# The fullest expert's overflow tokens in four 32-column tiles of plain fp32

## The reference

```python
def swiglu(x, w1, w3, w2):
    return (jax.nn.silu(x @ w1) * (x @ w3)) @ w2

def moe_ffn(x, router_w, w1, w3, w2):
    logits = (xt @ router_w).astype(F32)
    top_v, top_i = lax.top_k(logits, TOP_K)          # 2 of 8
    top_w = jax.nn.softmax(top_v, axis=-1)
    gates = jnp.sum(jax.nn.one_hot(top_i, N_EXPERTS) * top_w[..., None], axis=1)
    for e in range(N_EXPERTS):
        y = y + gates[:, e:e + 1] * swiglu(xt, w1[e], w3[e], w2[e])
```

## Time and profile before

| | |
|---|---|
| median of three timed runs | 2315.66 us (2313.2 to 2319.87) |
| the profiled execution | 2320.57 us, span 2318.8 us |
| TensorE busy | 98% of the span, 11067 matmul records |
| VectorE, ScalarE busy | 79%, 60% |
| granted TensorE clock, mean | 0.994 |
| DMA | 584.16 MB, mean 252 GB/s |

### The profile page before, as it was taken

How to read it: one execution, slowest core, us unless ns; L and a number is a source line. 1 busy time by engine, 2 the same in 40 slices (tenths; PEclk the granted TensorE clock), 3 DMA queues, 4 the chain that set the end, 5 groups by cost and what they waited for, 6 DMA issues and landing times.

```text
span 2318.8 us, 29142 instructions
## 1 busy us (share of the span) xinstructions
PE 2275.0 (98%) x11067; PEld 1881.2 (81%) x11067; DVE 1824.6 (79%) x2368; ACT 1381.1 (60%) x1580; POOL 31.7 (1%) x44
## 2 busy tenths in 40 slices
PE   8999999999999999999999998999999999999998
PEld 7788887788888788787888876888888888888887
DVE  4965467899867788999899988899765579987655
ACT  4444443578856677788878884565544536644543
POOL 0000000000000000000000000000000000000000
PEclk9999998999999999999999999999999999999999
DMA  8366553699977799999999995644566565355663
GB/s 277 118 209 189 184 167 124 259 348 401 388 245 259 273 341 346 338 409 413 408 373 408 413 413 209 193 128 153 177 195 190 181 202 167 116 184 174 194 187 122
DMA packets 198506, 584.16 MB, mean 252 GB/s; under 512 B 17260, under 2 KB 26616, under 8 KB 183641
## 3 DMA queue, kind: packets, MB, share of 16 engines
q1 hardware_dynamic: 196060, 573.97, 70.4%
q0 software_dynamic: 1872, 6.82, 0.8%
q10 hardware_dynamic: 428, 1.45, 0.2%
HBM read 580.07 MB, written 2.12 MB: 251 GB/s over the span
## 4 chain that ended last, share of the span: by engine, by line
PE 85%; DVE 9%; ACT 2%; issue 2%; DMA 1%; SPq 0%; POOL 0%; DVEq 0%; POOLq 0%; ACTq 0%
PE tile L1051 19%; PE tile L1053 19%; PE tile L1052 19%; PE tile L1572 5%; PE tile L1573 4%; PE aux L1174 3%; DVE units_parts L2578 3%; PE aux L1051 2%; PE aux L1053 2%; PE aux L1052 2%; PE aux L1573 1%; PE aux L1572 1%; PE aux L1543 1%; PE aux L1471 1%; PE aux L1852 1%
## 5 line engine op out<-in xcount | busy, mean ns | idle before, releaser
L2578 DVE TENSOR_TENSOR units_parts<-units,high 128x1024 fp32r<-128x1024 f32 (+3 forms) x339 | 482.5, 1441 | 88.8 <-ACT high L1980 85.9
L1052 PE MATMUL tile<-units_parts,acts 128*128 128x512 f32 (+2 forms) x1344 | 514.9, 383 | 0.0
L1980 ACT ACTIVATE high<-units 128x1024 fp32r<-128x1024 f32 (+3 forms) x339 | 412.4, 1236 | 150.8 <-DMA units<-in_w_ff 42.0
L1051 PE MATMUL tile<-high,acts 128*128 128x512 f32 (+2 forms) x1012 | 402.4, 398 | 5.8 <-DVE units_parts L2578 3.4
L1053 PE MATMUL tile<-high,acts 128*128 128x512 f32 (+2 forms) x1012 | 389.7, 385 | 0.0
L1052 PEld LDWEIGHTS tile<-units_parts,acts 128*128 128x128 f32 x1344 | 254.1, 189 | 47.1 <-issue 2.2
L1051 PEld LDWEIGHTS tile<-high,acts 128*128 128x128 f32 x1012 | 191.4, 189 | 44.1 <-issue 5.5
L1053 PEld LDWEIGHTS tile<-high,acts 128*128 128x128 f32 x1012 | 191.0, 189 | 38.6
L1052 PE MATMUL tile<-units_parts,zbuf_parts 128*128 128x512 f32 x328 | 127.6, 389 | 0.0
L1572 PE MATMUL tile<-high,params_parts 128*128 128x512 f32 x276 | 109.2, 396 | 0.4 <-ACT gbuf L2191 0.4
L1573 PE MATMUL tile<-units_parts,params_parts 128*128 128x512 f32 x276 | 107.7, 390 | 0.0
(11 more groups left out here) (560 smaller groups left out, 5181.9 us busy)
## 6 DMA issues: line engine op xcount, KB each, us to landing
units<-in_moe_w SPq DMA_DIRECT2D x156, 1024.0 KB, 8.2
units<-in_w_in SPq DMA_DIRECT2D x134, 512.0 KB, 3.8
units<-in_w_ff SPq DMA_DIRECT2D x128, 512.0 KB, 3.7
q_buf<-in_moe_w SPq DMA_DIRECT2D x39, 1024.0 KB, 8.5
k_buf<-in_moe_w SPq DMA_DIRECT2D x39, 1024.0 KB, 8.0
nat<-in_moe_w SPq DMA_DIRECT2D x39, 1024.0 KB, 8.7
bias<-in_moe_w SPq DMA_DIRECT2D x39, 1024.0 KB, 8.9
units<-in_ffn_w SPq DMA_DIRECT2D x48, 512.0 KB, 3.7
```

The source lines that it names most:

```text
L1051: nc.tensor.matmul(bank, lhs[0], high, start=start, stop=False)
L1052: nc.tensor.matmul(bank, lhs[0], low, start=False, stop=False)
L1980: nc.scalar.activation(high_slot(SG[0], n) if wide_ else high_slot(SG[0], n)[:, 0:cols], halves(weights) if wide_ else weights[:, 0:cols], ...
L2578: V.tensor_tensor(low, weights, high, ALU.subtract).then_inc(SG[0].low_ready, 1)
```

## The change

The fullest expert's overflow is now at most 32 tokens (`THIN`), so its round takes 160 tokens. These are no longer split. They meet the raw fp32 weights of a unit in plain fp32 matmuls: the four chunks of a unit go to four column tiles of the array, 32 columns each, and to four groups of 32 partitions of one PSUM bank. The sum over the four groups is made where the two halves were added before. Since VectorE writes the remainder over the raw weights, the products with a unit come before its split, three units ahead of the unit's other products; VectorE waits for them (`thin_done`). The overflow's second-matrix results, two halves of 512 columns and two chunks each, fill one bank; the final scatter adds the partitions, with the unused quarters of `large_ye` cleared. The overflow tokens are gathered as high plus low part in one bank (`gather_bank`), in another order of the eight gathers.

```diff
-CAP, FEW = P, P // 2
+CAP, FEW, THIN = P, P // 2, P // 4
...
+                    def thin_tiles(bank, lhs, weights, start, stop):
+                        for c, (rows_, of) in enumerate(zip(lhs, weights)):
+                            at = slice(c * THIN, (c + 1) * THIN)
+                            mm = nc.tensor.matmul(bank[at, :], rows_, of, start=start, stop=stop,
+                                                  tile_position=(0, c * THIN))
+                        return mm
+
+                    def thin_unit(i):
+                        weights, _, loaded, loads = slot(S, len(STREAM1) + large_at[i])
+                        pe.wait_ge(loaded, 16 * loads)
+                        if i < FIRST_UNITS:
+                            (t,), m, k, _ = first_place(LARGE, i)
+                            if i == 0:
+                                spare_done("gathered", LARGE - 1, 4)
+                                spare_done("gathered", LARGE - 1, 6)
+                            if k == 0:
+                                take_bank(2 + m, thin_raw_ready, 2 * t + m + 1)
+                            chunks = weights.rearrange("p (c n) -> p c n", c=EXPERT_CHUNKS)
+                            mm = thin_tiles(tiles[2 + m], [thin_x[:, EXPERT_CHUNKS * k + c, :] for c in range(EXPERT_CHUNKS)],
+                                            [chunks[:, c, :] for c in range(EXPERT_CHUNKS)], k == 0, k == TILE_UNITS - 1)
+                        else:
+                            k = i - FIRST_UNITS
+                            if k == 0:
+                                take_bank(2, ye_ready, outputs_before(LARGE) + 1)
+                            if k % 2 == 0:
+                                pe.wait_ge(few_added, k // 2 + 1)
+                            chunks = weights.rearrange("p (c h n) -> p c h n", c=EXPERT_ROWS, h=2)
+                            at = [(c, h) for h in range(2) for c in range(EXPERT_ROWS)]
+                            mm = thin_tiles(tiles[2], [thin_hidden[:, EXPERT_ROWS * k + c, :] for c, _ in at],
+                                            [chunks[:, c, h, :] for c, h in at], k == 0, k == BACK_UNITS - 1)
+                        mm.then_inc(thin_done, 1)
+
+                    def thin_ahead():
+                        reach = C.unit.n - len(STREAM1) + EXPERT_LEAD
+                        while C.thin.n < MOE_UNITS and large_at[C.thin.n] <= reach:
+                            thin_unit(C.thin.take())
...
                     def first_unit(r, i):
 
+                        thin_ahead()
...
-                                if r == LARGE:
-                                    mm = products_few(tiles[2 + m], both[:, at_k, :], high[:, row_, at],
-                                                      low[:, row_, at], start, stop)
...
                     def back_unit(r, k):
 
-                        out_first = outputs_before(r) + (2 if r == LARGE else 0)
+                        thin_ahead()
+                        out_first = outputs_before(r) + (1 if r == LARGE else 0)
...
-                        if r == LARGE:
-                            for h in range(2):
-                                at = slice(h * 512, (h + 1) * 512)
-                                for c in range(EXPERT_ROWS):
-                                    chunk = EXPERT_ROWS * k + c
-                                    mm = products_few(tiles[2 + h], large_hidden(chunk)[:, 0, :], high[:, c, at],
-                                                      low[:, c, at], chunk == 0, chunk == D_FFE // P - 1)
...
+                            for own in both:
+                                first = i * width + own.start - columns.start
+                                for b in range(TB):
+                                    mm = nc.tensor.matmul(bank[:, first:first + THIN], rest[:, b, at],
+                                                          chosen[:, b, own], start=False, stop=(b == TB - 1))
...
+                    def thin_out():
+                        reach = C.unit.n - 1 - len(STREAM1) + EXPERT_LEAD
+                        while C.thin.n < 2 * MOE_TILES and large_at[TILE_UNITS * C.thin.n + TILE_UNITS - 1] <= reach:
+                            n = C.thin.take()
+                            t, m = divmod(n, 2)
+                            act.wait_ge(thin_done, TILE_UNITS * (n + 1))
+                            if t > 0:
+                                turned = spare_at["raw", LARGE, t - 1, m]
+                                act.wait_ge(spare_evac[turned % 2], turned // 2 + 1)
+                            nc.scalar.activation(in_order(thin_raw[m]), pairs_of(tiles[2 + m]),
+                                                 ACT.Copy).then_inc(thin_raw_ready, 1)
...
                     dve.wait_ge(SG[0].high_ready, n + 1)
+                    if expert_unit(SG[0], n) in large_at:
+                        dve.wait_ge(thin_done, large_at.index(expert_unit(SG[0], n)) + 1)
...
-                V.tensor_scalar(caps[:, :, large:large + 1], caps[:, :, large:large + 1], float(FEW), None, ALU.add)
+                V.tensor_scalar(caps[:, :, large:large + 1], caps[:, :, large:large + 1], float(THIN), None, ALU.add)
...
+                    if r == LARGE + 1 and i == 0:
+                        V.memset(large_ye, 0.0).then_inc(large_cleared, 1)
```

More of the change, by code:

```diff
@@ L59 @@
 ROUNDS = N_EXP + EXTRA
+THIN_TILES = P // THIN
 assert SEQ <= CAP + 2 * FEW and 2 * SEQ // (MANY + 1) <= 2 * FEW
@@ L260, in lots, with thin, gather_order, bank_lots @@
         return [(4 * FEW, FEW, column_of(r), False, 1) if r >= N_EXP else (FEW, FEW, column_of(r), False, int(r == LARGE + 3))]
-    return [(2 * FEW, CAP, column_of(r), True, 0)] + ([(4 * FEW, FEW, ROUNDS, False, 1)] if r == LARGE else [])
+    return [(2 * FEW, CAP, column_of(r), True, 0)] + ([(4 * FEW, THIN, ROUNDS, False, 1)] if r == LARGE else [])
+def thin(lot):
+    return lot[1] == THIN
+def gather_order(r):
+    return (0, 2, 4, 6, 1, 3, 5, 7) if any(map(thin, gathered_lots(r))) else tuple(range(8))
+def bank_lots(r, i):
+    return [lot for lot in gathered_lots(r) if i == 0 or not thin(lot)]
 def gathered_lots(r):
@@ L284, in outputs_before @@
 def outputs_before(r):
-    return 2 * r + (2 if r > LARGE else 0)
+    return 2 * r + (1 if r > LARGE else 0)
 def few_before(r):
-    return sum(few(q) or q == LARGE for q in range(r))
+    return sum(few(q) for q in range(r))
 def column_of(r):
@@ L309, in step_units, with large_units @@
     return units
+def large_units():
+    stream = [unit for s in range(N_EXP + 1) for unit in step_units(s)]
+    at = [n for n, (r, _) in enumerate(stream) if r == LARGE]
+    assert [stream[n][1] for n in at] == list(range(MOE_UNITS))
+    return at
 def back_after(s, i):
@@ L366, in added_after @@
     if r == LARGE:
-        return [i // 4 - 1] if i >= 6 and i % 4 == 2 else []
+        return [i // 4] if i % 4 == 2 else []
     return [i // 4 - 2 + i % 8 - 1] if r == LARGE + 1 and i >= 9 and i % 8 in (1, 2) else []
 def lows_after(r, i):
-    if i < 2 or not (few(r) or r == LARGE):
+    if i < 2 or not few(r):
         return []
@@ L557, in gathered @@
             _, _, _, many, place = lot
+            if thin(lot):
+                return [thin_x]
             return gathered_many if many else [gathered_few[place][:, :, i * FEW:(i + 1) * FEW] for i in range(2)]
@@ L1462, in _, with gather_bank @@
                     keep_busy(3)
-                    def gather_bank(bank, part, chosen, lots_, j):
+                    def gather_bank(bank, part, chosen, lots_, j, rest=None):
                         columns = gather_columns(lots_)
                         width = columns.stop - columns.start
+                        both = [slice(lot[0], lot[0] + lot[1]) for lot in lots_ if thin(lot)]
                         for i in range(2):
@@ L1471, in gather_bank @@
                                 mm = nc.tensor.matmul(bank[:, i * width:(i + 1) * width], part[:, b, at],
-                                                      chosen[:, b, columns], start=(b == 0), stop=(b == TB - 1))
+                                                      chosen[:, b, columns], start=(b == 0),
+                                                      stop=(b == TB - 1 and not both))
+                            for own in both:
[3 more added lines that the diff above has]
+                                                          chosen[:, b, own], start=False, stop=(b == TB - 1))
                         return mm
@@ L3170, in add_halves @@
                 silu, linear = product_of(r, t)
-                V.tensor_tensor(silu, silu, linear, ALU.mult).then_inc(few_added, 1)
+                V.tensor_tensor(thin_hidden[:, 4 * t:4 * t + 4, :] if r == LARGE else silu, silu, linear,
+                                ALU.mult).then_inc(few_added, 1)
             def low_few(r, t):
                 dve.wait_ge(few_high, C.few_turned.take() + 1)
-                high, low = hidden_few(r, t)
```

(1 more changed line is left out.)

94 lines of the change are left out of this document (43 added, 51 removed).

## The result

| | before | after |
|---|---|---|
| device time, median of 6 runs | 2311.32 us (2309.07 to 2319.87) | 2296.14 us (2291.09 to 2299.32) |
| the profiled execution | 2320.57 us, span 2318.8 | 2291.09 us, span 2289.1 |

The ratio is 0.9927, with a 95% interval from 0.9907 to 0.9947. The change made the kernel faster by 12 to 21 us. The forecast was 2293 us.

A forecast was written before the change was run, and what follows sets the result against it. TensorE, busy 98% of the span, was taken to bound the touched steps: -24.0 us from 42 thin units and +1.0 for gathering make -23.0, from a median of 2315.66 to 2293 us. Range 2281 to 2329.

The forecast's parts named there:

- The mechanism: TensorE, fullest expert's overflow: four column tiles run side by side, eight passes in two slots of 0.4285, 0.857 us a unit.
- The size of a thin unit: TensorE, per unit: 0.857 us plus 0.19 in and 0.20 out, 1.25 us, replacing 1.82; 24.0 us gained over 42 units.
- The gathering: Before the fullest expert's units: 16 more small fp32r matmuls for the overflow's low parts, 1 us added, bounds 0 and 1.8.
- Step 1: Expert-phase stretch from 526.1 us, before the fullest expert's units; 107.5 us long, with 1 us added for gathering.
- steps 2 and 3: Fullest expert's first matrices, then its second between round 3's first: TensorE-bound, 16.0 and 8.0 us saved, to 157 and 125.
- three added waits: TensorE for raw loads, VectorE's split for thin products, ScalarE emptying thin banks: nothing, the last up to 3 us.
- VectorE's share: Fullest expert's second matrix between round 3's first: VectorE needs about 112 us of 124.6, share 0.90, which does not bind.
- The total: Whole kernel: -24.0 from the units and +1.0 from gathering, -23.0 us.
- gain half given back: Rival: four tiles overlap, but VectorE or ScalarE falls behind or TensorE waits early, losing half the gain; 2304 us, chance 0.10.

The follow-up runs named there:

- one tile: Against the changed kernel, all four chunks of a unit go to the first column tile, one after another; 2404.64 us.
- two tiles: Against the changed kernel, the four chunks of a unit go to two column tiles in turn; 2330.27 us.
- the full array: Against the changed kernel, one plain fp32 matmul of all 128 columns per unit, no column tiles, wrong overflow products; 2283.94 us.
- a pair: Changed kernel with third bank and later activation and product in round 3, plus thin products of two first-matrix units done together; 2291.89 us.
- the kernels with the later product: Changed kernel with a third bank and ScalarE's activation and VectorE's product one unit later in round 3, 2291.89 us; also with paired thin units, 2291.89 us.

## Why the prediction came out right

**The mechanism.** "I take it that four do as well: two slots of 0.4285." Right, and shown three ways: by the eight passes in after, and by eight, four and two slots with one tile, two tiles and the full array. The prediction took the step from two to four tiles without a row; the records now have it in all 42 units. The Trainium skill (TensorE: Matmul & The Clock Gate, Part 3, section Measured speedup vs the span model) has 3.07 for four tiles packed by rows. That figure, for row tiles, does not carry over to these column tiles: eight slots, 3.43 us, against 0.857 in the trace, a factor of 4.0.

**The size of a thin unit.** 1.25 us forecast, 1.20 measured. Coming out is 0.203 as the pooling means had it; going in is 0.139 where I had averaged 0.15 and 0.24 to 0.19. The gain of 42 units was thus 26.1 us and not 24.0.

**The gathering.** 1 us forecast. Step 1 has 0.7 us beyond its three thin units. The low parts stand there as 16 matmuls of their own, 32 columns wide:

```profile
L1509 PE MATMUL aux<-sc_parts,x_sb_parts x16: 215/240/263, 582.0 to 593.5; 128*128 128x32 f32 x16
```

**The steps.** 157 and 125 us forecast for steps 2 and 3, 156.1 and 125.6 measured. That is better than the reasoning deserves. The prediction left 28 and 14 thin units in their steps; three ran in step 1 and one crossed from step 3 to step 2, as the code says (reach is three units). For step 1 it had one us more for the gathering, 108.5, and not the 111.8 that came. DMA in step 2 was forecast at 285 GB/s and is 288.

**The waits.** This is the step that failed. I put all three added waits at nothing, and these three did cost little: the rows show no wait of TensorE for a thin bank or a load. But I asked only what the change adds, and not which wait that is there already loses its cover when TensorE becomes faster. The waits for round 3's banks (0.8 us in before, 4.5 after) and for the spare bank at 642.12 (1.6 us) do not come from the change's new semaphores. Together TensorE's waits in steps 2 and 3 rose by 4.8 us (3.1 to 7.9). I had written that TensorE would be the bound of step 3 because VectorE's share there is only 0.90. A share over 125 us says nothing about the last 12.4 us of the step, in which ScalarE waits for VectorE, VectorE for ScalarE and TensorE for both.

Of 6.7 us given back the rows name 5.5: 4.8 of waits and 0.7 in step 1. The rest, 1.2 us, is open. The starts of fp32r matmuls in step 3 lie slightly further apart than before (229.4 ns in the mean against 228.2), which makes about half of it; what causes that was not tried.

**The total.** -23.0 forecast, -19.4 in the steps. The error of +2.1 in the unit and the error of the waits went opposite ways. The forecast of 2293 us lies 3 us under the median of 2296.14 and inside the spread of the runs. Part of that is luck. The forecast started from 2315.66 us, the median of three runs of before, and over six runs it is 2311.32. The medians differ by 15.2 us and the interval ends at 21, so a gain of 23 us was too much, in the timed runs as in the steps. The part of "gain half given back" came true to a quarter: its mechanism, an engine that falls behind in step 3, is what happened, its size was too large.

**What stays open.** Whether the 1.6 us at 642.12 goes when the first raw results are turned a unit later was not tried. Nor was it tried whether the price of the changes of form is the two loads that nothing hides. The part ahead of the experts took 431.7 to 442.3 us in the eight profiles. The two long ones, before and the one-tile kernel, are the two that have 20.5 us at half clock there; why the clock fell in these two and not in the others stays open.

## What to carry to other kernels

Count column tiles by the slots of the fullest tile and add the change of form (here 0.14 us in and 0.20 us out) for each visit, not for each matmul; then put as many tiled matmuls as possible into one visit. When an engine at 98% loses work, look for the waits that its own work used to cover: list each wait on the next engines in the stretch, with its slack, before calling the saved time a gain. Compare steps bounded by the same instruction in both traces, because two whole spans can differ by 10 us before the change begins, 7.7 of them here by one stretch at half clock. And before moving an instruction behind another engine's next task, look who waits for it: here a product done one unit later cost 3.6 us of ScalarE.

## What the runs showed of the hardware

Four plain fp32 matmuls on four 32-column tiles run at the price of one: eight passes of 512 columns in 0.857 us, each with a moving operand of its own with 128 partitions. Passes on different tiles overlap although the program names them tile by tile, and passes on one tile do not (3.55 us for eight).

A weight load of 32 columns takes 106 to 109 ns and one of 128 columns 186 to 188. Of the eight loads of a thin unit only the first can show beside the two slots, and in the second unit of a pair none does (0.858 us). I had not expected that from loads that all go to the same rows of the array.

The change of form is not symmetric, 0.139 us in and 0.203 us out over the 42 units, and between two thin units in a row it is absent (0.858 us from end to end, 0.857 of it the slots).

The granted clock stood at half (the 1.2 GHz level) for 20.5 us in two of eight profiles at the same place of the program, and with it the stretch between two splits took 34.8 us in place of 27.1. It also fell to half for 3.4 us behind a wait of 3.14 us of TensorE (the kernels with the later product), and behind one of 2.17 us in the one-tile and two-tile kernels, but not behind one of 2.64 us in after.
